# A decoder layer in fp32 on one core: order of the operands and the squares in the first projection, a second head in free PSUM banks, and page loads ahead of the V loads

## The chip, the core and the metric

The kernel runs on one core of a Trainium2 chip. Its engines are TensorE (PE, with its weight loads shown as PEld), VectorE (DVE), ScalarE (ACT), GpSimd (POOL) and SyncE (SP), which here only issues transfers. The metric is device time in microseconds (us) for one launch. Lower is better.

## The reference, cut to what matters

One inference step of one hybrid layer, for 512 prompt rows and 64 sample rows (8 sequences of 8), 576 columns in all in the kernel's layout:

```
z = rmsnorm(x, g_pre_mix) @ w_in                 # 2048 -> 5120: u, va, q, k, vb
u, va, q, k, vb = split(z)
a_out = gelu(u) * (w_s @ rmsnorm(gelu(va)) + b_s)
lam   = exp(sum(lq1*lk1)) - exp(sum(lq2*lk2)) + lam_init
o     = (softmax(q1 k1) - lam * softmax(q2 k2)) @ v      # prompt; samples read 16 cache pages each
mix   = concat(a_out, rmsnorm(o)) @ w_out
h     = x + rmsnorm(mix)
y     = h + rmsnorm((gelu(gate) * val) @ w_down)         # gate, val: conv of rmsnorm(h) @ w_up
```

rmsnorm needs the sum of squares of each column of x. The kernel multiplies the weights with the unscaled x (times the gain) and divides the product by the root R afterwards, so the squares are needed only when the first product leaves PSUM.

## The kernel before

Each fp32 operand is split into a high part (ACT, a copy to fp32r) and a low part (the rest). A product is three matmuls: high by high, low by high, high by low. For the input x there are 16 tiles of 128 rows, `xraw` -> `xh` (ACT, L767) and `xl` (DVE, L1285). A weight unit holds 8 tiles of 128 by 128. It is loaded into one of two `wraw` slots, its high part `wh` is written by ACT (L754 for the first four units, `w_split_hi` L392 later) and its low part `wl` by POOL (L1181 to L1186, `w_split_lo` L397). `unit_mm` (L412 to L414) is one unit: 8 tiles, two column halves, three matmuls, 48 in all. A head's q takes two units (0 and 1 for head 0), its k takes the next two (2 and 3), head 1 takes units 4 to 7, and so on for 8 heads; then come the V units, then eight batches.

The first stage. SP issues unit 0, then x in five parts (`X_PARTS`: 2, 2, 4, 4 and 4 tiles), with the constants `cs` and the lambda rows `lamin` after the first part and units 1 and 2 after the second and fourth. `cs` and `lamin` raise one semaphore, `c_landed`, and ACT and DVE wait for both. ACT makes the high parts of part q, then the squares of part q-1 (L761), then the high part of a unit. DVE makes the low parts of part q, then adds the squares of part q-1 (L1279). There are two buffers for squares, so ACT's square k waits for DVE's add k-2. The sum goes through TensorE (`sum_squares`, L1872) between units 2 and 3, ACT takes the root (L787), DVE the reciprocal (L1298). DVE then evacuates q (L1306) and k (L1309) of head 0 from banks 0 to 3, and TensorE begins head 1 in those same banks. ACT's order in `qk_act` is fixed: after q's evacuation it copies the sample columns (L794), and only then splits units 6 and 7. SP stores q after the evacuation and only then issues the load of unit 7.

The pages. `pg` has 8 slots. Page n of a batch waits until TensorE has used the page 8 places before it. In batch 0 TensorE runs `k_pages(0)`, a half unit, `k_pages(1)`, a half unit, then `k_pages(2)` (L1917), which needs pages 8 to 11; each `k_pages` is followed by the scores of the prompt (L1940). SP's order around that point:

```
v_loads(3, first_page=4)
sp.wait_ge(v_stored[0], 16 * H)
sp.wait_ge(v_stored[1], 16 * H)
token_loads(sp, sy, 0)      # ws, wb, V, vnew
bias_load(sp, sy, 0)        # bsb
batch_loads(0)              # pages 8 to 31, then 0 to 7 of the next batch
```

Of the kernel before, what the change touches and what calls it, by code (L numbers as in the profile page):

```python
# [37 lines left out]
P = 128  # L38
# [122 lines left out]
def build(nc, xT, wstream, kpages, vpages, state, ptab, consts, lams, wsT, wblk, bs,  # L161
# [56 lines left out]
    kT = sb("kT", [P, SEQ], at=c)  # L218
    qb = sb("qb", [P, H, 32], at=c)
    knew = sb("knew", [P, H, DT], at=c)  # L220
    loaded_early = c[0]
    V = sb("V", [P, 4, P], at=c)
    vnew = sb("vnew", [DT, H * P], at=c)
    ws = sb("ws", [P, P], at=c)
    wb = sb("wb", [NS, NS], at=c)
    bsb = sb("bsb", [P, P], at=c)
    S = sb("S", [P, PAGES * P + DT], at=c)
    En = sb("En", [DT, P], at=c)
    W = sb("W", [P, 1280], at=c)
# [92 lines left out]
    w_landed = [sem(f"w_landed{i}") for i in range(RAW + 2)]  # L322
    w_hi, w_lo, w_used = sem("w_hi"), sem("w_lo"), sem("w_used")

    c_landed, p_landed, ready = sem("c_landed"), sem("p_landed"), sem("consts_ready")
    x_landed = [sem(f"rows_landed{i}") for i in range(len(X_PARTS))]
    r_landed = x_landed[:4]
# [164 lines left out]
        q.dma_start(knew[:].rearrange("p h n -> p (h n)"),  # L492
                    ks_d[:, bass.ds(j, 1), :].rearrange("p a n -> p (a n)")).then_inc(sq_landed, 16)

    def token_loads(eng, q, j):

        wait_past(eng, s["gm_ready"], j)
        q.dma_start(ws[:], wsT[bass.ds(j, 1)].rearrange("a p n -> (a p) n")).then_inc(g_landed, 16)
        q.dma_start(wb[:], wblk[bass.ds(j, 1)].rearrange("a p n -> (a p) n")).then_inc(g_landed, 16)
        wait_past(eng, s["pv_ready"], j)  # L500
        q.dma_start(V[:], v_out[bass.ds(j, 1)].rearrange("a b p n -> p (a b) n")).then_inc(hv_landed, 16)
        wait_past(eng, s["spv_ready"], j)
        q.dma_start(vnew[:], vs_out[bass.ds(DT * j, DT)].rearrange("t h n -> t (h n)")).then_inc(sv_landed, 16)
# [10 lines left out]
    def _(sp):  # L514
# [7 lines left out]
        for q, (k0, k1) in enumerate(X_PARTS):  # L522
            sp.dma_start(xraw[:, k0:k1, :], xT[:, k0:k1, :]).then_inc(x_landed[q], 16)
            if q == 0:
                sp.dma_start(cs[:], consts).then_inc(c_landed, 16)
                sp.dma_start(lamin[:], lams.to_broadcast([P, 4, DH])).then_inc(c_landed, 16)
            if q in FIRST_UNITS:
                first_load(FIRST_UNITS[q])
        for u in (3, 4):
            first_load(u)  # L530

# [40 lines left out]
        sp.wait_ge(p_landed, 16)  # L572
        v_loads(2, first_page=0)
        head_loads(sp, sy, 0)
        v_loads(3, first_page=4)

        sp.wait_ge(v_stored[0], 16 * H)
        sp.wait_ge(v_stored[1], 16 * H)
        token_loads(sp, sy, 0)
        bias_load(sp, sy, 0)  # L580

        def batch_loads(j, last=False):
            for n in range(8, 12):
                page(n, j)
            for n in range(12, 24):
                page(n, j)
            for c in range(1, 3):
                for n in range(20 + 4 * c, 24 + 4 * c):
                    page(n, j)
            if not last:  # L590
                for n in range(8):
                    page(n, j + 1)
# [158 lines left out]
    def _(act):  # L751
# [2 lines left out]
            sc.activation(wh[:, u, :], wraw[:, u % RAW, :], ACT.Copy).then_inc(w_hi, 1)  # L754

        first_split_hi(0)
        act.wait_ge(c_landed, 32)
        def x_squares(k0, k1):
            for k in range(k0, k1):
                wait_past(act, x_acc, k - 1)  # L760
# [2 lines left out]
        for q, (k0, k1) in enumerate(X_PARTS):  # L763
            act.wait_ge(x_landed[q], 16)
            for k in range(k0, k1):

                sc.activation(xh[:, k, :], xraw[:, k, :], ACT.Copy, scale=cs[:, C_PRE + k:C_PRE + k + 1]  # L767
                              ).then_inc(x_hi, 1)
            if q:
                x_squares(*X_PARTS[q - 1])  # L770
            if q in FIRST_UNITS:
                first_split_hi(FIRST_UNITS[q])
            if q == 4:

                act.wait_ge(lam_sum, 2)
                sc.activation(lt[:, 2:4], lt[:, 0:2], ACT.Exp).then_inc(lam_exp, 1)
        first_split_hi(3)
        x_squares(*X_PARTS[-1])

        def qk_act(j):  # L780

            for t in range(2):
                w_split_hi(U_QK, 4 * t, 8, j)
                w_split_hi(U_QK, 4 * t + 1, 8, j)
                if type(j) is int and t == 0:
                    act.wait_ge(ssq_mm, 1)
                    sc.activation(halves(R[:]), tile_out(6), ACT.Sqrt, scale=1.0 / D, bias=EPS  # L787
                                  ).then_inc(sq_root, 1)
                act.wait_ge(q_evac, 2 * j + t + 1)
                act.wait_ge(pool_c, 2)  # L790
                for z in range(2):

                    o = 2 * DT * t + DT * z
                    sc.activation(  # L794
                        qbd[DH * z:DH * z + DH, :, bass.ds(2 * j + t, 1), o:o + DT].rearrange("p b a n -> p b (a n)"),
                        zt[0][DH * z:DH * z + DH, SEQ:T].rearrange("p (b n) -> p b n", b=DB),
                        ACT.Copy).then_inc(smp, 1)
                w_split_hi(U_QK, 4 * t + 2, 8, j)
# [13 lines left out]
        def batch(j, first=False, last=False):  # L812
# [46 lines left out]
            sc.activation(vq[:], vg[:], ACT.Square).then_inc(s["vsq_ready"], 1)  # L859

            wait_past(act, s["vaT_ready"], j)
            act.wait_ge(c_landed, 32)
            sc.activation(vaT[:], vg[:], ACT.Copy, scale=cs[:, bass.ds(C_VA + j, 1)]).then_inc(s["va_gained"], 1)
            act.wait_ge(s["vssq_ready"], j + 1)
            sc.activation(vr[:, 0:4], pb[:, 3, SSQ_COL:SSQ_COL + 4], ACT.Sqrt, scale=1.0 / HD, bias=EPS
# [15 lines left out]
            act.wait_ge(s["sss_ready"], j + 1)  # L881
            sc.activation(osq[:], pb[:, 4, 0:NS], ACT.Sqrt, scale=1.0 / HD, bias=EPS).then_inc(s["ssd_done"], 1)
            if not last:
                token_loads(act, sc, j + 1)
            act.wait_ge(s["u_evac"], j + 1)
            sc.activation(ug[:], ug[:], ACT.Gelu_apprx_tanh).then_inc(s["ugelu"], 1)
# [49 lines left out]

        def out_copy(t, m):

            act.wait_ge(c_landed, 32)
            sc.activation(mix_half(t, m), out_bank(t, m), ACT.Copy, scale=cs[:, C_POST + m:C_POST + m + 1]  # L940
                          ).then_inc(m_copied, 1)

# [107 lines left out]
        def conv_tap2(n, t):  # L1050
# [7 lines left out]
            act.wait_ge(ub_zero, 4)  # L1058
            act.wait_ge(st_in, 2 * n + 2 - t)
            wait_past(act, gv_done, n)  # L1060
            act.wait_ge(c_landed, 32)
            f_ = n + KF * t
            sc.activation(cv[t][:, 0:NC_], ubs[n % 2][t][:, 2:UB], ACT.Identity,
                          scale=cs[:, C_W + 4 * KF + f_:C_W + 4 * KF + f_ + 1],
# [196 lines left out]

    @block.vector
    def _(dve):
        dve.wait_ge(c_landed, 32)

        for z in range(2):
            v.tensor_tensor_reduce(out=lamin[:, 2 * z, :], in0=lamin[:, 2 * z, :], in1=lamin[:, 2 * z + 1, :],
                                   scale=1.0, scalar=0.0, op0=ALU.mult, op1=ALU.add,
                                   accum_out=lt[:, z:z + 1]).then_inc(lam_sum, 1)
        ch = Chain(dve, dve_c, 0)  # L1270
        ch.link(v.tensor_scalar(gsub[:], cs[:, C_SUB:C_SUB + 1], 1.0 - LAM_INIT, None, ALU.mult))
        def add_x_squares(k0, k1):
# [8 lines left out]
        for q, (k0, k1) in enumerate(X_PARTS):  # L1281
            dve.wait_ge(x_landed[q], 16)
            for k in range(k0, k1):
                dve.wait_ge(x_hi, k + 1)
                v.scalar_tensor_tensor(out=xl[:, k, :], in0=xraw[:, k, :], scalar=cs[:, C_PRE + k:C_PRE + k + 1],  # L1285
                                       in1=xh[:, k, :].bitcast(F32), op0=ALU.mult, op1=ALU.subtract
                                       ).then_inc(x_lo, 1)
            if q:
                add_x_squares(*X_PARTS[q - 1])
        add_x_squares(*X_PARTS[-1])  # L1290
        dve.wait_ge(lam_exp, 1)

        ch.link(v.tensor_tensor(lt[:, 0:1], lt[:, 3:4], lt[:, 2:3], ALU.subtract))
        ch.link(v.tensor_scalar(neglam[:], lt[:, 0:1], -LAM_INIT, None, ALU.add))
        ch.link(v.tensor_scalar(sgn[:], cs[:, C_SEL + 1:C_SEL + 2], neglam[:, 0:1], None, ALU.mult))
        ch.link(v.tensor_tensor(sgn[:], sgn[:], cs[:, C_SEL:C_SEL + 1], ALU.add))
        dve.wait_ge(sq_root, 1)
        v.reciprocal(R[:], R[:]).then_inc(R_ready, 1)  # L1298
        dve.wait_ge(R_ready, 1)
        Rh = halves(R[:])  # L1300

        def qk_evac(j):
            tile_done(dve, U_QK, 0, 4, j)
            wait_past(dve, q_stored, 16 * j)
            wait_past(dve, smp, 3 * j)
            v.tensor_tensor(halves(zt[0][:]), tile_out(0), Rh, ALU.mult).then_inc(q_evac, 1)  # L1306
            tile_done(dve, U_QK, 2, 4, j)
            wait_past(dve, k_stored, 16 * j)
            v.tensor_tensor(halves(zt[1][:]), tile_out(2), Rh, ALU.mult).then_inc(k_evac, 1)  # L1309

        qk_evac(0)
        with dve.Fori(1, H) as j:
            qk_evac(j)
        dve.wait_ge(q_stored, 16 * H)
        dve.wait_ge(k_stored, 16 * H)
# [548 lines left out]
    def _(pe):  # L1864
# [9 lines left out]
            m.then_inc(ssq_mm, 1)  # L1874

        tile_mm(0, U_QK, 0, k_sem=x_lo)
        unit_mm(2, U_QK, 2, xh, xl, 0, 8, True, False).then_inc(w_used, 1)
        sum_squares(6, (x_acc, KD, acc0))
        unit_mm(2, U_QK, 3, xh, xl, 8, 8, False, True).then_inc(w_used, 1)
        with pe.Fori(1, H) as j:  # L1880
            wait_past(pe, q_evac, j)
            tile_mm(0, U_QK, 0, 4, j)
            wait_past(pe, k_evac, j)
            tile_mm(2, U_QK, 2, 4, j)
# [440 lines left out]
```

## Time and profile before

| | us |
|---|---|
| median of three runs | 2623.59 (2622.09 to 2625.20) |
| the profiled execution, its own time | 2626.07 |
| its span, first to last instruction | 2624.3 |
| PE busy | 2536.9 (97% of the span) |
| DVE busy | 1463.3 (56%) |
| ACT busy | 1014.6 (39%) |
| POOL busy | 731.2 (28%) |
| load of one weight unit, issue to landing | 3.7 |

The mean granted TensorE clock is 0.990 of full speed. Positions below are us from the start of the span. A matmul of 288 columns starts 0.13 us after the one before it at the full clock of 2.4 GHz and 0.24 us after it at 1.2 GHz. In a timeline the bracket behind a row gives the idle time of the engine ahead of it and what ended it.

### The profile page before, as it was taken

The numbers are of one execution on the slowest core, as the hardware profiler recorded it, in microseconds if no ns is written. First come the engines' busy times: TensorE is split into PE (matmuls) and PEld (weight loads), VectorE is DVE, ScalarE is ACT, GpSimd is POOL, SyncE is SP. The second block draws the span as 40 slices with busy tenths as digits, with TensorE's granted clock in tenths as the row PEclk, the third lists the DMA queues.
The fourth block names the chain that finished last, engine by engine and source line by source line (L and its number), as shares of the span: only waits on it lengthen the run. The fifth ranks groups of instructions, "written<-read, shape, count | busy, mean of one in ns | idle before, by whom it ended". The sixth has DMA issues, their size and how long they took to land.

```text
span 2624.3 us, 49612 instructions
## 1 busy us (share of the span) xinstructions
PE 2536.9 (97%) x19608; PEld 2419.4 (92%) x19608; DVE 1463.3 (56%) x2100; ACT 1014.6 (39%) x1478; POOL 731.2 (28%) x547
## 2 busy tenths in 40 slices
PE   7999989999999999899999999999999999999997
PEld 6999967777778998899999999999999999999997
DVE  5000134445545378988888888888888302131347
ACT  5111133444444454444444444444444222222342
POOL 3333321212215500111111111111111433335774
PEclk9999999999999999999999999999999999999998
DMA  5333579999996663233333333333333442424654
GB/s 177 105 105 120 157 291 347 354 366 367 365 362 242 202 198 117 95 110 107 105 105 108 111 106 111 111 111 111 104 110 136 151 135 81 155 87 128 222 157 153
DMA packets 147367, 445.02 MB, mean 170 GB/s; under 512 B 17216, under 2 KB 39232, under 8 KB 145536
## 3 DMA queue, kind: packets, MB, share of 16 engines
q1 hardware_dynamic: 130608, 413.26, 46.7%
q10 hardware_dynamic: 15024, 24.70, 2.6%
q0 software_dynamic: 1568, 4.72, 0.4%
q8 instruction: 119, 1.95, 0.3%
q14 instruction: 48, 0.39, 0.0%
HBM read 406.05 MB, written 36.33 MB: 169 GB/s over the span
## 4 chain that ended last, share of the span: by engine, by line
PE 88%; DVE 5%; DMA 3%; issue 2%; SPq 1%; ACT 1%; ACTq 0%; POOL 0%; DVEq 0%; POOLq 0%
PE pb L2187 12%; PE pb L2189 12%; PE pb L2188 12%; PE pb L2213 7%; PE pb L2216 7%; PE pb L2215 7%; PE pb L412 6%; PE pb L414 5%; PE pb L413 5%; PE pb L2101 3%; PE pb L2103 3%; PE pb L2102 3%; PE pb L1981 2%; PE pb L1917 2%; DMA pg<-in_kpages 1%
## 5 line engine op out<-in xcount | busy, mean ns | idle before, releaser
L2187 PE MATMUL pb<-reg,uh 128*128 128x288 f32 x2408 | 713.2, 296 | 12.7 <-DVE reg L1576 5.4
L2189 PE MATMUL pb<-reg,ul 128*128 128x288 f32 x2408 | 711.9, 296 | 0.0
L2188 PE MATMUL pb<-reg,uh 128*128 128x288 f32 x2408 | 708.3, 294 | 0.0
L1035 ACT ACTIVATE uh<-ua 128x1024 fp32r<-128x1024 f32 x301 | 318.0, 1057 | 436.2 <-PE pb L2189 206.3
L2187 PEld LDWEIGHTS pb<-reg,uh 128*128 128x128 f32 x2408 | 452.8, 188 | 14.2 <-issue 10.8
L2188 PEld LDWEIGHTS pb<-reg,uh 128*128 128x128 f32 x2408 | 455.6, 189 | 0.0
L2189 PEld LDWEIGHTS pb<-reg,ul 128*128 128x128 f32 x2408 | 453.9, 188 | 0.0
L1637 DVE TENSOR_TENSOR ul<-ua,uh 128x1024 fp32r<-128x1024 f32 x301 | 367.4, 1221 | 103.6 <-ACT uh L1035 103.5
L412 PE MATMUL pb<-xh,wh 128*128 128x288 f32 x1280 | 387.1, 302 | 19.7 <-DVE xl L1285 18.5
L413 PE MATMUL pb<-xl,wh 128*128 128x288 f32 x1280 | 379.1, 296 | 0.0
L414 PE MATMUL pb<-xh,wl 128*128 128x288 f32 x1280 | 378.2, 295 | 0.0
L1259 POOL TENSOR_TENSOR ul<-ua,uh 128x1024 fp32r<-128x1024 f32 x120 | 291.8, 2440 | 288.9 <-ACT uh L1119 288.1
L397 POOL TENSOR_TENSOR wl<-wraw,wh 128x1024 fp32r<-128x1024 f32 x80 | 191.4, 2394 | 488.2 <-ACT wh L392 488.2
L2213 PE MATMUL pb<-xl,uh 128*128 128x288 f32 x1024 | 303.5, 296 | 4.1 <-POOL ul L1259 4.1
L2215 PE MATMUL pb<-xh,uh 128*128 128x288 f32 x1024 | 302.5, 295 | 0.0
L2216 PE MATMUL pb<-xl,ul 128*128 128x288 f32 x1024 | 302.0, 295 | 0.0
L1240 POOL COPY hs<-ub 128x2 f32<-128x2 f32 x88 | 52.9, 601 | 791.0 <-DVE ub L1698 631.6
L412 PEld LDWEIGHTS pb<-xh,wh 128*128 128x128 f32 x1280 | 242.1, 189 | 31.2 <-issue 23.4
L1119 ACT ACTIVATE uh<-ua 128x1024 fp32r<-128x1024 f32 x120 | 127.0, 1059 | 354.0 <-PE pb L2216 333.3
L414 PEld LDWEIGHTS pb<-xh,wl 128*128 128x128 f32 x1280 | 242.4, 189 | 0.0
L413 PEld LDWEIGHTS pb<-xl,wh 128*128 128x128 f32 x1280 | 242.2, 189 | 0.1
L392 ACT ACTIVATE wh<-wraw 128x1024 fp32r<-128x1024 f32 x80 | 84.8, 1059 | 320.4 <-PE pb L414 307.6
(254 smaller groups left out, 4368.9 us busy)
## 6 DMA issues: line engine op xcount, KB each, us to landing
ua<-in_wstream SPq DMA_DIRECT2D x292, 512.0 KB, 3.8
pg<-in_kpages SPq DMA_DIRECT2D x128, 512.0 KB, 5.7
pg<-in_vpages SPq DMA_DIRECT2D x128, 512.0 KB, 5.9
wraw<-in_wstream SPq DMA_DIRECT2D x82, 512.0 KB, 3.7
wraw<-in_wstream ACTq DMA_DIRECT2D x32, 512.0 KB, 6.3
wmore<-in_wstream SPq DMA_DIRECT2D x30, 512.0 KB, 3.9
g_d<-gv SPq DMA_DIRECT2D x44, 288.0 KB, 2.1
xh<-g_d SPq DMA_DIRECT2D x8, 1152.0 KB, 9.9
```

The costliest lines, as they stand in the source:

```text
L412: te.matmul(pb[:, bank + n, 0:TH], whk, hn, start=a0, stop=False)
L413: te.matmul(pb[:, bank + n, 0:TH], whk, ln, start=False, stop=False)
L414: m = te.matmul(pb[:, bank + n, 0:TH], wlk, hn, start=False, stop=z0)
L1035: sc.activation(uh[q % SLOTS][:], ua[src][:], ACT.Copy).then_inc(u_hi, 1)
L1259: pl.tensor_tensor(ul[dn_slot(q)][:], ua[DN_RAW[q % 4]][:], uh[dn_slot(q)][:].bitcast(F32), ALU.subtract).then_inc(u_lo, 1)
L1637: v.tensor_tensor(ul[q % SLOTS][:], ua[src][:], uh[q % SLOTS][:].bitcast(F32), ALU.subtract).then_inc(u_lo, 1)
L2187: te.matmul(out, whk, xhk, start=opens and k == 0, stop=False, skip_group_check=again)
L2188: te.matmul(out, whk, xlk, start=False, stop=False, skip_group_check=again)
L2189: m = te.matmul(out, wlk, xhk, start=False, stop=k == HK - 1, skip_group_check=again)
L2213: te.matmul(pb[:, b_ + n, 0:TH], whk, gh_[:, k, n * TH:(n + 1) * TH], start=r == r0 and kk == 0, stop=False)
L2215: te.matmul(pb[:, b_ + n, 0:TH], whk, gl_[:, k, n * TH:(n + 1) * TH], start=False, stop=False)
L2216: m = te.matmul(pb[:, b_ + n, 0:TH], wlk, gh_[:, k, n * TH:(n + 1) * TH], start=False, stop=r == r1 - 1 and kk == GRP - 1)
```

## The change

1. `lamin` gets a semaphore of its own, `lam_landed`, and its load is issued behind all of x. `c_landed` now stands for `cs` alone.
2. ACT makes the high parts of all 16 tiles of x (with units 1 and 2 between them), then squares 0 and 1, unit 3, squares 2 to 11, unit 4, squares 12 to 15, then the exponentials of lambda. DVE makes all low parts, then adds all squares, then does the lambda sums (L1267), the reciprocal of R, and the four small lambda operations (L1293 to L1296).
3. TensorE puts head 1 into banks 4 to 7. Its order is units 0 to 4, the sum of the squares (through banks 6 and 7), unit 5, a wait for the root, units 6 and 7; only head 2 returns to bank 0. `qk_evac` gets the bank as a parameter.
4. `ws`, `wb` and `bsb` move to the part of SBUF that is free early. `gate_loads` (ws, wb) and `bias_load` of batch 0 are issued ahead of `v_loads(3)`. Pages 8 to 11 are issued ahead of the wait for the V stores and the loads of `V` and `vnew`.

```diff
             sp.dma_start(xraw[:, k0:k1, :], xT[:, k0:k1, :]).then_inc(x_landed[q], 16)
             if q == 0:
                 sp.dma_start(cs[:], consts).then_inc(c_landed, 16)
-                sp.dma_start(lamin[:], lams.to_broadcast([P, 4, DH])).then_inc(c_landed, 16)
             if q in FIRST_UNITS:
                 first_load(FIRST_UNITS[q])
+        sp.dma_start(lamin[:], lams.to_broadcast([P, 4, DH])).then_inc(lam_landed, 16)
...
         v_loads(2, first_page=0)
         head_loads(sp, sy, 0)
+        gate_loads(sp, sy, 0)
+        bias_load(sp, sy, 0)
         v_loads(3, first_page=4)
-        sp.wait_ge(v_stored[0], 16 * H)
-        sp.wait_ge(v_stored[1], 16 * H)
-        token_loads(sp, sy, 0)
-        bias_load(sp, sy, 0)
         def batch_loads(j, last=False):
             for n in range(8, 12):
                 page(n, j)
+            if type(j) is int and j == 0:
+                sp.wait_ge(v_stored[0], 16 * H)
+                sp.wait_ge(v_stored[1], 16 * H)
+                token_loads(sp, sy, 0)
             for n in range(12, 24):
                 page(n, j)
...
-            if q:
-                x_squares(*X_PARTS[q - 1])
             if q in FIRST_UNITS:
                 first_split_hi(FIRST_UNITS[q])
-            if q == 4:
-                act.wait_ge(lam_sum, 2)
-                sc.activation(lt[:, 2:4], lt[:, 0:2], ACT.Exp).then_inc(lam_exp, 1)
+        x_squares(0, 2)
         first_split_hi(3)
-        x_squares(*X_PARTS[-1])
+        x_squares(2, 12)
+        w_split_hi(U_QK, 0)
+        x_squares(12, KD)
+        act.wait_ge(lam_sum, 2)
+        sc.activation(lt[:, 2:4], lt[:, 0:2], ACT.Exp).then_inc(lam_exp, 1)
...
-            if q:
-                add_x_squares(*X_PARTS[q - 1])
-        add_x_squares(*X_PARTS[-1])
+        add_x_squares(0, KD)
+        dve.wait_ge(lam_landed, 16)
+        for z in range(2):
+            v.tensor_tensor_reduce(...).then_inc(lam_sum, 1)
+        dve.wait_ge(sq_root, 1)
+        v.reciprocal(R[:], R[:]).then_inc(R_ready, 1)
         dve.wait_ge(lam_exp, 1)
...
         qk_evac(0)
-        with dve.Fori(1, H) as j:
+        qk_evac(1, 4)
+        with dve.Fori(2, H) as j:
             qk_evac(j)
...
         tile_mm(0, U_QK, 0, k_sem=x_lo)
-        unit_mm(2, U_QK, 2, xh, xl, 0, 8, True, False).then_inc(w_used, 1)
+        tile_mm(2, U_QK, 2)
+        unit_mm(4, U_QK, 4, xh, xl, 0, 8, True, False).then_inc(w_used, 1)
         sum_squares(6, (x_acc, KD, acc0))
-        unit_mm(2, U_QK, 3, xh, xl, 8, 8, False, True).then_inc(w_used, 1)
-        with pe.Fori(1, H) as j:
+        unit_mm(4, U_QK, 5, xh, xl, 8, 8, False, True).then_inc(w_used, 1)
+        pe.wait_ge(sq_root, 1)
+        tile_mm(6, U_QK, 6)
+        with pe.Fori(2, H) as j:
```

## Rows read from the trace of the kernel before

**Rows 1.** Timeline of PE, first stage: start, duration, line, [idle before <- releaser].

```profile
11.28 0.58 PE L412 MATMUL pb<-xh,wh 128*128 128x288 f32 x1 [11.28 <-DVE xl L1285]
...
30.37 0.61 PE L412 MATMUL pb<-xh,wh 128*128 128x288 f32 x1 [4.91 <-DVE xl L1285]
...
42.20 1.13 PE L1872 MATMUL pb<-acc,ones 128*128 128x288 f32 x4
...
49.95 0.40 PE L412 MATMUL pb<-xh,wh 128*128 128x288 f32 x1 [0.25 <-DVE zt L1306]
...
62.71 0.29 PE L414 MATMUL pb<-xh,wl 128*128 128x288 f32 x1
```

**Rows 2.** Busy time of each engine by stretch, two stretches with the granted clock.

```profile
28.35:35.18 6.83, 4.81 (x20) 4.81 (x21) 6.52 (x8) 4.53 (x9) 1.36 (x1) 0.50 0.29 79
...
357.20:362.90 5.70, 5.68 (x23) 1.70 (x24) 0.41 (x1) 0.60 (x1) 0.00 (x0) 0.50 0.76 297
```

**Rows 3.** Timeline of PE around batch 0's page waits and batch 1's.

```profile
342.41 0.37 PE L1940 MATMUL pb<-kT,qT 64*128 64x128 f32 x1
...
357.21 3.64 PE L1917 MATMUL pb<-pg,qb 128*32 128x512 f32 x16 [5.05 <-DMA pg<-in_kpages]
...
418.15 1.92 PE L1917 MATMUL pb<-pg,qb 128*32 128x512 f32 x16 [2.19 <-DMA pg<-in_kpages]
```

**Rows 4.** DMA from 0 to 60 us: GB/s in 1.5 us slices, issues with time to landing.

```profile
GB/s 0 128 356 381 101 287 441 432 430 430 405 436 425 383 145 0 0 0 0 0 85 265 11 0 0 0 115 235 5 0 259 90 0 32 231 270 56 194 316 3
...
cs<-in_consts SPq DMA_DIRECT2D x1, 217.5 KB, 4.9
lamin<-in_lams SPq DMA_DIRECT2D x1, 128.0 KB, 7.0
```

**Rows 5.** The last part of x, line L523: its issue, and its time to landing.

```profile
L523 SPq DMA_DIRECT2D xraw<-in_xT x1: 442/442/442, 8.6 to 8.6; - x1
...
DMA to landing us min/median/max: 13.1/13.1/13.1
```

**Rows 6.** Timeline of ACT, first stage.

```profile
9.39 2.88 ACT L767 ACTIVATE xh<-xraw,cs 128x576 fp32r<-128x576 f32 x4 [3.56 <-DMA lamin<-in_lams]
...
26.24 1.04 ACT L754 ACTIVATE wh<-wraw 128x1024 fp32r<-128x1024 f32 x1
...
44.52 0.65 ACT L787 ACTIVATE R<-pb 128x576 f32<-128x576 f32 x1
49.85 0.53 ACT L794 ACTIVATE qbd<-zt 64x64 f32<-64x64 f32 x2 [4.68 <-DVE zt L1306]
```

**Rows 7.** Timeline of DVE, first stage.

```profile
24.00 3.34 DVE L1279 TENSOR_TENSOR acc<-acc,sq 128x576 f32<-128x576 f32 x4
28.04 4.46 DVE L1285 SCALAR_TENSOR_TENSOR xl<-xraw,cs,xh 128x576 fp32r<-128x576 f32 x4 [0.71 <-ACT xh L767]
...
45.27 3.75 DVE L1298 RECIPROCAL R<-R 128x576 f32<-128x576 f32 x1 [1.36 <-ACT R L787]
```

**Rows 8.** Timeline of POOL, first stage.

```profile
27.35 2.35 POOL L1186 TENSOR_TENSOR wl<-wraw,wh 128x1024 fp32r<-128x1024 f32 x1 [10.53 <-ACT wh L754]
...
51.54 2.40 POOL L397 TENSOR_TENSOR wl<-wraw,wh 128x1024 fp32r<-128x1024 f32 x1 [5.29 <-ACT wh L392]
```

**Rows 9.** Timeline of PE: two idle gaps in the feed-forward stage and the matmuls behind them.

```profile
1077.28 0.37 PE L2187 MATMUL pb<-reg,uh 128*128 128x288 f32 x1 [2.78 <-DVE reg L1576]
...
1084.17 0.58 PE L2187 MATMUL pb<-reg,uh 128*128 128x288 f32 x1 [3.47 <-DVE u L1687]
```

**Rows 10.** Timeline of SP's queue at the start of batch 0.

```profile
345.51 1.53 SPq L508 DMA_DIRECT2D bsb<-in_bs  x1
348.00 8.08 SPq L563 DMA_DIRECT2D pg<-in_kpages  x8
```

**Rows 11.** Busy time by stretch, batches 1 and 2: PE, PEld, DVE, ACT, POOL, clock, DMA share, GB/s.

```profile
392.80:451.30 58.50, 54.95 (x507) 41.75 (x506) 27.35 (x66) 23.97 (x54) 11.62 (x9) 1.00 0.95 353
451.30:507.90 56.60, 54.96 (x507) 41.76 (x506) 27.46 (x66) 23.98 (x54) 11.58 (x9) 1.00 0.96 366
```

More of the change, by code:

```diff
@@ L220, in build @@
     knew = sb("knew", [P, H, DT], at=c)
+    ws = sb("ws", [P, P], at=c)
+    wb = sb("wb", [NS, NS], at=c)
+    bsb = sb("bsb", [P, P], at=c)
     loaded_early = c[0]
@@ L223, in build @@
     vnew = sb("vnew", [DT, H * P], at=c)
-    ws = sb("ws", [P, P], at=c)
-    wb = sb("wb", [NS, NS], at=c)
-    bsb = sb("bsb", [P, P], at=c)
     S = sb("S", [P, PAGES * P + DT], at=c)
@@ L323, in build @@
     w_hi, w_lo, w_used = sem("w_hi"), sem("w_lo"), sem("w_used")
+    lam_landed = sem("lam_landed")
     c_landed, p_landed, ready = sem("c_landed"), sem("p_landed"), sem("consts_ready")
@@ L493, in head_loads, with gate_loads @@
                     ks_d[:, bass.ds(j, 1), :].rearrange("p a n -> p (a n)")).then_inc(sq_landed, 16)
-    def token_loads(eng, q, j):
+    def gate_loads(eng, q, j):
         wait_past(eng, s["gm_ready"], j)
@@ L499, in token_loads @@
         q.dma_start(wb[:], wblk[bass.ds(j, 1)].rearrange("a p n -> (a p) n")).then_inc(g_landed, 16)
+    def token_loads(eng, q, j):
         wait_past(eng, s["pv_ready"], j)
@@ L756, in _ @@
         first_split_hi(0)
-        act.wait_ge(c_landed, 32)
+        act.wait_ge(c_landed, 16)
         def x_squares(k0, k1):
@@ L768, in _ @@
                               ).then_inc(x_hi, 1)
-            if q:
-                x_squares(*X_PARTS[q - 1])
             if q in FIRST_UNITS:
                 first_split_hi(FIRST_UNITS[q])
-            if q == 4:
-                act.wait_ge(lam_sum, 2)
-                sc.activation(lt[:, 2:4], lt[:, 0:2], ACT.Exp).then_inc(lam_exp, 1)
+        x_squares(0, 2)
         first_split_hi(3)
-        x_squares(*X_PARTS[-1])
+        x_squares(2, 12)
[3 more added lines that the diff above has]
+        sc.activation(lt[:, 2:4], lt[:, 0:2], ACT.Exp).then_inc(lam_exp, 1)
         def qk_act(j):
             for t in range(2):
-                w_split_hi(U_QK, 4 * t, 8, j)
+                if type(j) is not int or t:
+                    w_split_hi(U_QK, 4 * t, 8, j)
                 w_split_hi(U_QK, 4 * t + 1, 8, j)
@@ L861, in batch @@
             wait_past(act, s["vaT_ready"], j)
-            act.wait_ge(c_landed, 32)
+            act.wait_ge(c_landed, 16)
             sc.activation(vaT[:], vg[:], ACT.Copy, scale=cs[:, bass.ds(C_VA + j, 1)]).then_inc(s["va_gained"], 1)
@@ L883, in batch @@
             if not last:
+                gate_loads(act, sc, j + 1)
                 token_loads(act, sc, j + 1)
@@ L937, in out_copy @@
         def out_copy(t, m):
-            act.wait_ge(c_landed, 32)
+            act.wait_ge(c_landed, 16)
             sc.activation(mix_half(t, m), out_bank(t, m), ACT.Copy, scale=cs[:, C_POST + m:C_POST + m + 1]
@@ L1060, in conv_tap2 @@
             wait_past(act, gv_done, n)
-            act.wait_ge(c_landed, 32)
+            act.wait_ge(c_landed, 16)
             f_ = n + KF * t
@@ L1263, in _ @@
     def _(dve):
[L1264 to L1269, printed above, removed]
+        dve.wait_ge(c_landed, 16)
         ch = Chain(dve, dve_c, 0)
@@ L1287, in _ @@
                                        ).then_inc(x_lo, 1)
-            if q:
-                add_x_squares(*X_PARTS[q - 1])
-        add_x_squares(*X_PARTS[-1])
+        add_x_squares(0, KD)
+        dve.wait_ge(lam_landed, 16)
+        for z in range(2):
+            v.tensor_tensor_reduce(out=lamin[:, 2 * z, :], in0=lamin[:, 2 * z, :], in1=lamin[:, 2 * z + 1, :],
+                                   scale=1.0, scalar=0.0, op0=ALU.mult, op1=ALU.add,
+                                   accum_out=lt[:, z:z + 1]).then_inc(lam_sum, 1)
+        dve.wait_ge(sq_root, 1)
+        v.reciprocal(R[:], R[:]).then_inc(R_ready, 1)
         dve.wait_ge(lam_exp, 1)
@@ L1296, in _, with qk_evac @@
         ch.link(v.tensor_tensor(sgn[:], sgn[:], cs[:, C_SEL:C_SEL + 1], ALU.add))
-        dve.wait_ge(sq_root, 1)
-        v.reciprocal(R[:], R[:]).then_inc(R_ready, 1)
         dve.wait_ge(R_ready, 1)
         Rh = halves(R[:])
-        def qk_evac(j):
+        def qk_evac(j, bank_=0):
             tile_done(dve, U_QK, 0, 4, j)
@@ L1305, in qk_evac @@
             wait_past(dve, smp, 3 * j)
-            v.tensor_tensor(halves(zt[0][:]), tile_out(0), Rh, ALU.mult).then_inc(q_evac, 1)
+            v.tensor_tensor(halves(zt[0][:]), tile_out(bank_), Rh, ALU.mult).then_inc(q_evac, 1)
             tile_done(dve, U_QK, 2, 4, j)
             wait_past(dve, k_stored, 16 * j)
-            v.tensor_tensor(halves(zt[1][:]), tile_out(2), Rh, ALU.mult).then_inc(k_evac, 1)
+            v.tensor_tensor(halves(zt[1][:]), tile_out(bank_ + 2), Rh, ALU.mult).then_inc(k_evac, 1)
         qk_evac(0)
-        with dve.Fori(1, H) as j:
+        qk_evac(1, 4)
+        with dve.Fori(2, H) as j:
             qk_evac(j)
```

## The prediction, made before the changed kernel ran

> **What bounds the kernel now.** I read the page first: TensorE is busy 97% of the span, so only time in which it idles or runs at the lower clock can be won. Then I asked for TensorE's waits up to 90 us and around the start of the batches, and read each gap in the timelines. In the first stage TensorE starts at 11.28, stands still 4.91 us before 30.37 for the last part of x's low halves, and is then fed without a gap over 0.3 us: the two units of head 1 run from 49.95 to 62.71 [rows 1]. That is 96 matmuls, 0.134 us apart, so one unit is 6.4 us and unit 6 starts at 62.85. After the gap the clock is at the lower of its two levels, 1.2 of 2.4 GHz, until 35.18 [rows 2]. The second place is batch 0: `k_pages(2)` waits 5.05 us for page 11 and then takes 3.64 us instead of 1.92 [rows 3], with the clock at the lower level until 362.9 [rows 2]. These two places are what the change touches.
>
> **Parts 1 and 2, the first stage.** Each time is from the span's start.
>
> *Loads.* The first high part waited for `lamin` from 5.83 to 9.39 [rows 6]; `cs`, issued 0.47 us before it, lands 2.1 us sooner relative to its own issue, so at about 6.75 [rows 4]. The first high part therefore moves to about 6.8: 2.6 us. For the later parts of x, what `lamin` holds up in the queue is between 0.3 us (its 128 KB at 430 GB/s) and 2.6 us (9.32 less 6.75, if nothing else landed meanwhile). The rate falls to 101 and 287 GB/s in the slices from 6 to 9 us [rows 4], which is 1.7 us lost plus the bytes: I take 2.0. The last part of x, issued at 8.65 and landed 13.1 us later [rows 5], comes at 19.7 instead of 21.75.
>
> *Operands.* ACT makes a tile's high part in 0.69 us and four in 2.8 [rows 6], so tiles 12 to 15 get theirs from 19.7 to 22.5, where before the first began at 27.18, behind squares and a unit split. Unit 2's split stands just before them, at 18.4, and POOL, which takes 2.35 for a low part [rows 8], runs it from 19.5 to 21.85. DVE collides with that: the four low parts that began at 28.04 ended 2.8 us after POOL's operation did [rows 7, 8], the first held until POOL was through. So DVE's last low part ends at 21.85 + 2.8 = 24.65, and TensorE's products with it at 25.5. The same point was at about 35.8 before (30.37 plus four tiles of 1.44 us at the lower clock, the last at the full one): 10.3 us sooner. Units 2 and 3 follow to 38.3.
>
> *Squares.* They are now behind all of that: the adds begin at 24.6. POOL's low part of unit 3 runs 24.65 to 27.0, and add 1 is held to 27.6. From there ACT and DVE alternate at 0.86 us (four adds in 3.34 [rows 7]); square 11, and behind it on ACT the split of unit 4, comes at 35.1, its low part is ready at 38.65. TensorE waits 0.3 us, nothing more. Unit 4 lasts to 45.05. The adds end at 41.7, hidden by it with 3.3 us to spare; the lambda sums and the exponential follow, and unit 5 is split by 45.85, just at its turn. With this cover gone (squares over 3.3 us later) every further us is a us of TensorE.
>
> *The root, and what is late next.* Before, the sum's matmuls started at 42.20 and unit 4 began 7.75 us later, of which unit 3 covered nearly all [rows 1]. Now: sum 45.05 to 46.2, root 0.65, reciprocal 3.75 [rows 6, 7], four small lambda operations about 0.8 that are now behind it, evacuation 0.76, ending at 52.4. But ACT waits for this evacuation before it copies sample columns (0.53, [rows 6]) and splits unit 6 (1.04), and POOL needs 2.40 after it [rows 8]: unit 6 can start at 56.5. TensorE has done unit 5 by 52.2. It waits about 3.8 us. Unit 7's load, behind the same evacuation on SP, lands 3.7 us after it and is split before unit 6 is through, so it costs nothing. Unit 6 moves from 62.85 to 56.5: 6.3 us.
>
> *The clock in that gap.* A gap of 3.47 us left the clock low (first matmul 0.58), one of 2.78 did not (0.37) [rows 9]; 3.8 is on the side of the first, as are 4.91 and 5.05. From 30.37 the lower level lasted to 35.18 and from 357.21 to 362.9, of which half is lost: 2.4 to 2.8 us. I take 2.6. The Trainium skill ("TensorE: Matmul & The Clock Gate", Part 1) says that the point at which the clock changes differs from run to run of one kernel; by that page the gap could also pass at the full clock, which is a rival below. Net for the first stage: 6.3 - 2.6 = 3.7 us.
>
> The collision of DVE and POOL has a page as well: the Trainium skill ("SBUF — State Buffer", SBUF: two separate sides) makes it an exclusive lock that goes to whoever started first, so that POOL would also wait for a DVE add with two inputs. The rows show only DVE waiting. By the page the low parts of units 3 and 4 could each start up to 0.76 us late, and the sum below would be 10.1 instead of 10.9.
>
> **Part 3.** Without the other banks unit 4 could not start before the evacuation; its cost is nil, since the matmuls are the same. Its gain is in the times above.
>
> **Part 4, batch 0.** SP issued the token and bias loads until 347.0 and pages 8 to 11 only from 348.00 [rows 10], though TensorE had used pages 0 to 3 at 342.4, where the scores behind them begin [rows 3]. Page 11 landed just before 357.2, 9.1 us after the first issue. Now the first goes out at 342.5, page 11 lands at about 351.6, and `k_pages(2)` is due at 352.1. The wait of 5.05 goes, and with it the lower clock: 1.7 us in `k_pages(2)` [rows 3] and about 0.8 in what follows it; half of the stretch of 5.70 at the lower clock [rows 2] would be 2.85, and I count 2.5. What moves: `V` and `vnew` are now behind four page issues and a wait for TensorE, 2 us later, and are needed only some 45 us on, at the start of the first stretch of [rows 11]; ws, wb and bsb add 2.4 us of SP time ahead of a V unit's load of 3.7, and TensorE takes 6.4 for a unit and has another in hand. Pages 12 to 15 are issued from 348.2, behind `V`, land by 357.5 and are due at 358.5. Lower bound 5.05 (clock stays low anyway), upper 7.55. I take 7.2, near the upper end, as the clock falls only with a gap.
>
> **Sum.** 3.7 + 7.2 = 10.9 us. The profiled execution took 2626.07, 1.8 over its span of 2624.3, and would take 2615.2; the median of the runs is 2623.6, so 2612.7. Everything behind the two places is fed by TensorE's own progress and shifts with it.
>
> **Rivals.**
>
> *The clock holds in the new gap* (20%): 6.3 + 7.2 = 13.5, time 2610.1. For it: 3.8 is close to 3.47. Against: none of the gaps from 3.47 up that I read left it high.
>
> *The batches give part of it back* (15%). DMA is busy 95% and moves 353 GB/s in batch 1 and 366 in batch 2, and batch 1 has a page wait of 2.19 [rows 3, 11]. If the pages cannot follow 7 us sooner, this wait grows to about 6 with a lower clock behind it: total gain 5 to 6, time 2618. For it: batch 1 is 1.9 us longer than batch 2. Against: batch 2 moves 366 GB/s where batch 1 moves 353, so the queue has room there.
>
> *The first stage gains nothing* (8%). Squares come over 3.3 us late, and unit 4 and the root with them; with 4 us of that, only part 4 is left: 2616.4.
>
> *Slower* (4%). The pages now run just behind their slots in every batch, and the wait before `k_pages(2)`, 2.19 in batch 1, passes the 3.5 us at which the clock falls. Each such batch costs about 3.5 more of waiting and 2.6 of clock, 6 in all. Two cancel the gain, three make it slower: 2631 with four. For it: DMA at 95%. Against: batch 2 shows what a batch settles to, 56.60 for 54.96 of work.
>
> The forecast itself has 50%, with 2611 to 2615 as its own range; 3% is for the rest.
>
> **How the numbers follow.** A measurement of this kernel can tell about 0.2%, 5.2 us, from no change. Faster than 2618.4: the forecast, the first and third case, most of the second: 0.87. Same: the rest of the second and a small gain: 0.08. Slower: 0.05. The range reaches below to the clock case less 1.6 us for the runs' own spread, 2608.5, and above past the second and third case, 2618.5.
>
> **What would show it.** TensorE starts near 8.9; its products with the last tile end at 25 to 26; it waits 3 to 5 us ahead of unit 6 for POOL's low part, starting that unit near 56.5, at the lower clock; no page wait at batch 0, whose third page group takes 1.92; batch 1's page wait at 1 to 3 us. The prediction is wrong if ACT's squares with POOL's locks run slower than 0.86 each, so that unit 4 waits by us, if the page waits grow, or if the gap ahead of unit 6 is much longer.

## The result, and the profile after

| | before | after |
|---|---|---|
| median of the runs, us | 2624.86 (6 runs, 2622.09 to 2626.18) | 2614.62 (6 runs, 2612.61 to 2616.43) |
| profiled execution, own time | 2626.07 | 2614.37 |
| its span | 2624.3 | 2612.4 |

By its median the changed kernel is 10.2 us faster. The ratio that was worked out from the runs is 0.9966, 95% interval 0.9956 to 0.9976, which is 8.9 us (6.3 to 11.5). The prediction was 2612.7, with 2608.5 to 2618.5 as its range, and faster. The kernel before was timed again beside the changed one, so its median here is 1.3 us above the one that the prediction started from. A later measurement (the last experiment) gave 0.9972, 0.9960 to 0.9983.

The timeline of TensorE in the first stage, changed kernel; the columns are those of [rows 1]:

```profile
8.80 0.58 PE L413 MATMUL pb<-xh,wh 128*128 128x288 f32 x1 [8.80 <-DVE xl L1286]
...
22.06 0.40 PE L413 MATMUL pb<-xh,wh 128*128 128x288 f32 x1 [1.32 <-DVE xl L1286]
...
38.56 0.40 PE L413 MATMUL pb<-xh,wh 128*128 128x288 f32 x1 [0.25 <-POOL wl L398]
...
45.06 1.13 PE L1877 MATMUL pb<-acc,ones 128*128 128x288 f32 x4
...
56.33 0.37 PE L413 MATMUL pb<-xh,wh 128*128 128x288 f32 x1 [3.76 <-POOL wl L398]
...
64.32 0.30 PE L413 MATMUL pb<-xh,wh 128*128 128x288 f32 x1
```

The 4.91 us ahead of the last part of x are 1.32. Units 0 to 4 are done where the sum of the squares starts, at 45.06; before, units 0 to 2 were done at 42.20. The new gap is where it was expected: 3.76 us ahead of unit 6, ended by POOL's low part. Unit 6 starts at 56.33 instead of 62.85, 6.5 us sooner; the last row is the start of unit 7.

The chain that ends in it, on ACT, DVE and POOL, from their timelines:

```profile
46.23 0.65 ACT L792 ACTIVATE R<-pb 128x576 f32<-128x576 f32 x1 [1.74 <-PE pb L1877]
52.16 0.53 ACT L799 ACTIVATE qbd<-zt 64x64 f32<-64x64 f32 x2 [5.27 <-DVE zt L1310]
52.71 1.06 ACT L393 ACTIVATE wh<-wraw 128x1024 fp32r<-128x1024 f32 x1
```

```profile
20.09 4.10 DVE L1286 SCALAR_TENSOR_TENSOR xl<-xraw,cs,xh 128x576 fp32r<-128x576 f32 x4 [0.95 <-ACT xh L772]
...
46.92 3.75 DVE L1296 RECIPROCAL R<-R 128x576 f32<-128x576 f32 x1 [4.91 <-ACT R L792]
```

```profile
18.95 2.44 POOL L1192 TENSOR_TENSOR wl<-wraw,wh 128x1024 fp32r<-128x1024 f32 x1 [5.85 <-ACT wh L759]
24.16 2.67 POOL L1192 TENSOR_TENSOR wl<-wraw,wh 128x1024 fp32r<-128x1024 f32 x1 [2.77 <-ACT wh L759]
...
53.84 2.34 POOL L398 TENSOR_TENSOR wl<-wraw,wh 128x1024 fp32r<-128x1024 f32 x1 [8.19 <-ACT wh L393]
```

The split of unit 6 (ACT, 52.71) stands behind the sample columns, which wait for the evacuation, and its low part ends at 56.2. ACT had been idle for 5.27 us before that.

The clock in and behind the gap (busy time by stretch, columns as in [rows 11]):

```profile
52.60:57.18 4.58, 0.85 (x6) 0.88 (x7) 0.18 (x1) 1.83 (x3) 2.34 (x1) 0.99 0.57 179
57.18:60.59 3.41, 3.41 (x17) 3.41 (x15) 0.76 (x1) 0.60 (x3) 2.37 (x1) 0.51 0.85 235
```

It fell, as forecast, but not within the gap: unit 6 runs at the upper level for its first 0.8 us and then at the lower one for 3.41 us, and not for 5. Unit 7 starts 7.99 us behind unit 6, where a unit takes 6.40 at the upper level: 1.6 us is lost. From there to the V units the changed kernel is 4.9 us ahead.

Batch 0, TensorE and then SP's queue (before: [rows 3, 10]):

```profile
347.50 1.92 PE L1925 MATMUL pb<-pg,qb 128*32 128x512 f32 x16 [0.28 <-DMA pg<-in_kpages]
...
354.47 1.92 PE L1925 MATMUL pb<-pg,qb 128*32 128x512 f32 x16 [0.76 <-DMA pg<-in_kpages]
```

```profile
336.24 0.55 SPq L558 DMA_DIRECT2D out_vs<-vt  x1
337.88 4.05 SPq L567 DMA_DIRECT2D pg<-in_kpages  x4
342.04 0.40 SPq L505 DMA_DIRECT2D V<-out_v  x1
342.48 0.51 SPq L507 DMA_DIRECT2D vnew<-out_vs  x1
343.98 3.69 SPq L567 DMA_DIRECT2D pg<-in_kpages  x4
```

The third page group waits 0.28 us instead of 5.05 and takes 1.92 instead of 3.64. It starts 9.7 us ahead of the kernel before, of which 4.9 came from the first stage; the fourth group starts 11.5 us ahead (354.47 instead of 366.02). By the start of the output projection the lead is 11.4 (table below).

### The profile page after: what moved, and what is told of

Its sections match the earlier page's. It is cut to its first block, busy times and chain, and to the rows that moved or that the text cites. A ratio compares the mean times of both kernels' runs of the same rounds, so it can differ in the third digit from the quotient of the medians.

```text
span 2612.4 us, 49600 instructions
## 1 busy us (share of the span) xinstructions
PE 2532.2 (97%) x19608; PEld 2417.1 (93%) x19608; DVE 1463.4 (56%) x2100; ACT 1015.6 (39%) x1478; POOL 731.4 (28%) x547
## 4 chain that ended last, share of the span: by engine, by line
PE 87%; DVE 4%; DMA 3%; issue 2%; SPq 1%; ACT 1%; POOL 1%; ACTq 0%; DVEq 0%; POOLq 0%
PE pb L2195 12%; PE pb L2197 12%; PE pb L2196 12%; PE pb L2221 7%; PE pb L2224 7%; PE pb L2223 7%; PE pb L413 5%; PE pb L415 5%; PE pb L414 5%; PE pb L2109 3%; PE pb L2111 3%; PE pb L2110 3%; PE pb L1989 2%; DMA pg<-in_kpages 2%; PE pb L1925 1%
```

## The experiments

Positions are from each run's own profile. "Lead" is by how much the first matmul of the output projection, the first work of TensorE behind the eight batches, comes sooner than in the kernel before. Each ratio is to the kernel before on the same chip. Its medians there were 2624.86 beside the changed kernel, 2623.65 beside the first four experiments, 2623.50 beside the next four and 2622.42 beside the last two. There is one profile of the kernel before, of an execution of 2626.07 us, which is 1.2 to 3.6 us above these medians; so leads come out larger than what the medians show.

| run | median | ratio, 95% interval | unit 6 starts | wait of page group 3 | lead |
|---|---|---|---|---|---|
| before | 2624.86 | | 62.85 | 5.05 | |
| after | 2614.62 | 0.9966 (0.9956 to 0.9976) | 56.33 | 0.28 | 11.4 |
| first stage alone | 2620.62 | 0.9988 (0.9979 to 0.9998) | 56.38 | 5.10 | 3.9 |
| batch 0 alone | 2617.52 | 0.9980 (0.9971 to 0.9989) | 62.60 | none | 8.9 |
| no gap | 2609.62 | 0.9945 (0.9932 to 0.9959) | 52.47 | 1.45 | 18.0 |
| one set of banks | 2620.98 | 0.9990 (0.9980 to 0.9999) | | none | 3.1 |
| banks alone, batch 0 changed | 2617.66 | 0.9978 (0.9968 to 0.9988) | 62.79 | 0.76 | 6.7 |
| lambda load back | 2616.33 | 0.9970 (0.9958 to 0.9982) | 58.82 | 0.21 | 10.0 |
| V ahead of the pages | 2618.48 | 0.9979 (0.9969 to 0.9988) | 56.67 | 4.04 | 9.2 |
| no gap, V later | 2607.50 | 0.9938 (0.9924 to 0.9952) | 52.81 | none | 15.8 |
| last part first | 2608.08 | 0.9946 (0.9933 to 0.9960) | 52.61 | 0.18 | 17.4 |
| after, once more | 2614.86 | 0.9972 (0.9960 to 0.9983) | 56.38 | 0.60 | 11.9 |

**First stage alone.** The changed kernel with the old order at batch 0.

```diff
         head_loads(sp, sy, 0)
-        gate_loads(sp, sy, 0)
-        bias_load(sp, sy, 0)
         v_loads(3, first_page=4)
+        sp.wait_ge(v_stored[0], 16 * H)
+        sp.wait_ge(v_stored[1], 16 * H)
+        gate_loads(sp, sy, 0)
+        token_loads(sp, sy, 0)
+        bias_load(sp, sy, 0)
...
-            if type(j) is int and j == 0:
-                sp.wait_ge(v_stored[0], 16 * H)
-                sp.wait_ge(v_stored[1], 16 * H)
-                token_loads(sp, sy, 0)
```

> The changed first stage with the order of loads of the kernel before at batch 0. Theory (the two parts add up, and each is worth what its place shows): TensorE as in the changed kernel up to the batches, 4.9 us ahead of the kernel before; batch 0's page wait back at about 5 us with the lower clock behind it, end 4.9 us before the kernel before's. Rival (the batches are bound by their transfers and swallow an earlier start of TensorE): the lead shrinks to under 2 us by the end of the batches.

The wait is back at 5.10 us, the clock falls behind it, and the lead of 4.9 survives that place. At the end of the batches it is 3.9: the theory holds with 1 us given back, which is more than nothing and far from the rival's "under 2". The runs' median is 3.0 us below the kernel before, with an interval from 0.5 to 5.5.

**Batch 0 alone.** The kernel before with only the page, gate and bias loads reordered.

> The first stage of the kernel before with the changed order of loads at batch 0. Theory: no lead until 340 us, then 6.5 us, 2 of it by the clock that no longer falls, and 6.5 at the end. Rival (most of the saved wait comes back later as a longer page wait in batch 1 or 2): a lead of 6.5 behind batch 0 and under 4 at the end of the batches.

Batch 0 is left with a lead of 8.0 and the output projection starts 8.9 sooner; the runs' median says 6.1 (forecast 6.5). The rival is out. The two parts together come to 9.2 us by the medians, the whole change to 10.2 and 7.6 in its two measurements: they add up, as far as this can tell.

**No gap.** ACT splits unit 6 and SP loads unit 7 ahead of their waits for q's evacuation.

```diff
                 w_split_hi(U_QK, 4 * t + 1, 8, j)
+                if first_head:
+                    w_split_hi(U_QK, 2, 8, j)
                 if type(j) is int and t == 0:
                     act.wait_ge(ssq_mm, 1)
...
+            if type(j) is int:
+                w_load(U_QK, 2, 4, j)
             sp.wait_ge(q_evac, j + 1)
```

> The changed kernel with ACT's split of unit 6 ahead of its wait for the evacuation of q of head 0, and SP's load of unit 7 ahead of the same wait. Theory (the 3.76 us ahead of unit 6 are the chain evacuation, sample columns, high part, low part, and the lower clock for 3.4 us behind it costs 1.7): both go, unit 6 starts at 52.2 and the kernel is 5.5 us faster than the changed one, 16 to 17 below the kernel before. Rival (the root comes late in any case and only moves the wait to unit 8, which needs head 0's evacuation): the gap moves behind unit 7, gain under 2 us.

ACT and POOL now do both units back to back while the sum of the squares goes on:

```profile
42.22 1.99 ACT L393 ACTIVATE wh<-wraw 128x1024 fp32r<-128x1024 f32 x2
```

```profile
43.34 4.75 POOL L398 TENSOR_TENSOR wl<-wraw,wh 128x1024 fp32r<-128x1024 f32 x2 [4.76 <-ACT wh L393]
```

Unit 6 starts at 52.47, straight behind unit 5; no gap comes behind unit 7 either, and the clock stays at the upper level to the end of the batches. Batch 0 starts 5.4 us ahead of the changed kernel, as forecast from 3.76 and 1.7 (the two are 3.86 and 1.6). The time is 14.0 us below the kernel before, against 10.2 and 7.6 for the changed one, and not 16 to 17. Part of that may be the third page group, which waits 1.45 us here: one issue of a V store takes SP 1.92 us instead of 0.6, and page 8 goes out 1.6 us after its slot is free. Why that issue took longer I have not found. The two moves, on ACT and on SP, were not tried apart.

**One set of banks.** The changed kernel with head 1 in banks 0 to 3 again.

```diff
         tile_mm(2, U_QK, 2)
-        unit_mm(4, U_QK, 4, xh, xl, 0, 8, True, False).then_inc(w_used, 1)
         sum_squares(6, (x_acc, KD, acc0))
-        unit_mm(4, U_QK, 5, xh, xl, 8, 8, False, True).then_inc(w_used, 1)
-        pe.wait_ge(sq_root, 1)
-        tile_mm(6, U_QK, 6)
-        with pe.Fori(2, H) as j:
+        with pe.Fori(1, H) as j:
...
         qk_evac(0)
-        qk_evac(1, 4)
-        with dve.Fori(2, H) as j:
+        with dve.Fori(1, H) as j:
```

> The changed kernel with head 1 back in banks 0 to 3: TensorE runs units 0 to 3, the sum of the squares, then unit 4 behind the evacuation. Theory (the second set of banks is what lets TensorE use its head start of 10 us): TensorE idles from 38 to about 42 for the adds and from 43 to 49.5 for the root, at the lower clock behind it, so unit 4 starts 0 to 1 us before where it did in the kernel before, and the first stage gains nothing; 6.5 us in all, from batch 0. Rival (the gain of the first stage is the earlier operands alone, the banks are incidental): 10 to 11 us as in the changed kernel.

```profile
41.92 2.29 PE L1876 MATMUL pb<-acc,ones 128*128 128x288 f32 x4 [3.45 <-DVE acc L1280]
50.68 0.60 PE L413 MATMUL pb<-xh,wh 128*128 128x288 f32 x1 [6.47 <-DVE zt L1310]
```

TensorE reaches the end of unit 3 some 11 us sooner than before and then has nothing to do: 3.45 us for the adds, 6.47 for the root. The rival is out. Unit 4 starts at 50.68, 0.7 us after its place in the kernel before, not 0 to 1 before it: I had not counted that the sum itself runs at the lower clock (2.29 us for 1.13). The lower clock lasts until 54.8, and unit 8 starts 2.6 us later than in the kernel before (78.22 for 75.65). The first stage has turned from a gain into a loss. Batch 0 gives 7.3 us, so that the lead is 4.8 behind its fourth page group, and 3.1 is left at the end of the batches. The runs' median is 2.7 us below the kernel before, and not 6.5.

**Banks alone.** The old order of loads, operands and squares, with head 1 in banks 4 to 7 and batch 0 as changed.

> The first stage of the kernel before in its order of loads, operands and squares, with only the second head in banks 4 to 7; batch 0's loads in the changed order. Theory (banks without the earlier operands save nothing but the 0.25 us ahead of unit 4, since TensorE reaches the end of unit 3 only when the root is nearly done): unit 6 starts 0 to 0.5 us ahead of the kernel before, the whole is as the run with batch 0's part alone, 6 us. Rival (the banks are the gain): 10 us.

Unit 6 starts at 62.79, as in the kernel before (62.85), and the median is 5.8 us lower, as with batch 0's part alone (6.1). The second set of banks by itself gives nothing, and the earlier operands without it less than nothing: the 6.5 us exist only together.

**Lambda load back.** The load of the lambda rows in its old place, with the new semaphore.

```diff
             if q == 0:
                 sp.dma_start(cs[:], consts).then_inc(c_landed, 16)
+                sp.dma_start(lamin[:], lams.to_broadcast([P, 4, DH])).then_inc(lam_landed, 16)
-        sp.dma_start(lamin[:], lams.to_broadcast([P, 4, DH])).then_inc(lam_landed, 16)
```

> The changed kernel with the lambda rows' load issued in its old place behind the constants, still with a semaphore of its own. Theory (the load holds the queue for 2.55 us): every part of x lands 2.5 us later than in the changed kernel, TensorE starts at most 1 us later but ends the products of the last tile and starts unit 6 2.5 us later, the kernel is 2.5 us slower than the changed one. Rival (only the common semaphore cost time): no difference.

Unit 6 starts at 58.82, 2.5 us later. The DMA rate in 1.5 us slices shows the hole, here and, below it, gone in the changed kernel:

```profile
GB/s 0 123 399 354 70 263 427 443 424 430 412 425 435 386 191 0 87 257 16 0 139 210 0 0 0 0 0 0 254 112 0 0 0 0 0 0 0 246 300 25
```

```profile
GB/s 0 142 355 410 407 443 442 406 436 390 445 430 193 272 19 268 82 0 38 292 19 0 0 0 0 0 87 273 5 0 0 0 0 0 0 202 257 87 147 290
```

From 6 to 9 us the rate is 70 and 263 GB/s with the load and 407 and 443 without it. A load of 128 KB, the same 1 KB row to 128 partitions, costs the queue 2.5 us, where its bytes at 430 GB/s would take 0.3. It is over a third of what unit 6 gained. The 2.5 us are read from the profile; the runs' medians, 7.2 us below the kernel before here and 10.2 and 7.6 for the changed kernel, cannot tell them.

**V ahead of the pages.** The wait for the V stores and the loads of V and vnew ahead of pages 8 to 11; the gate and bias loads stay early.

> The changed kernel with the wait for the V stores and the loads of V and vnew ahead of pages 8 to 11, as before; ws, wb and bsb stay early. Theory (each us by which page 8 is issued later is a us of TensorE at the third page group): page 8 goes out at 341 instead of 337.9, TensorE waits 3 to 3.5 us there, and if the clock falls 2.5 more; 3 to 6 us slower than the changed kernel. Rival (the early gate and bias loads were the gain): under 1 us slower.

The pages go out at 342.08 instead of 337.88, the third group waits 4.04 us and the clock falls. So the place of the pages is the gain, not the early gate loads. By the medians 5.0 us of the gain is left, where the changed kernel has 10.2 and 7.6: it costs some 3 to 5 us. The lead at the end of the batches is only 2.2 below the changed kernel's, since this profile has nearly no page waits in the later batches. TensorE's waits for pages from 365 to 800 us (us in total, times, longest), this kernel and then the changed one with the first stage alone:

```profile
PE pb L1925 <- DMA pg<-in_kpages: 0.5, 2, 0.3
```

```profile
PE pb L1925 <- DMA pg<-in_kpages: 4.7, 8, 1.4
```

**No gap, V later.** V and vnew behind page 15.

```diff
-            for n in range(12, 24):
+            for n in range(12, 16):
                 page(n, j)
+            if type(j) is int and j == 0:
+                sp.wait_ge(v_stored[0], 16 * H)
+                sp.wait_ge(v_stored[1], 16 * H)
+                token_loads(sp, sy, 0)
+            for n in range(16, 24):
+                page(n, j)
```

> The kernel without the gap ahead of unit 6, and in batch 0 V and vnew behind page 15. Theory (pages 12 to 15 come 1 us sooner, so the wait ahead of the fourth page group goes): that wait, 0.4 to 0.8, is zero; 0.5 us better than without the move, which the runs' times cannot tell but the profile can. Rival (the pages are bound by the transfer rate, V's 0.26 MB must come in any case): the wait stays or moves to the V pages.

The wait ahead of the fourth group stays, 0.59 us: the rival is right, the move does nothing that can be seen. (The third group does not wait here, since page 8 goes out 0.3 us after its slot is free.) The kernel is the fastest by its median, 16.0 us below the kernel before, and cannot be told from the one without the move.

**Last part first.** On top of that, other places for three unit splits on ACT.

```diff
-            if q in FIRST_UNITS:
-                first_split_hi(FIRST_UNITS[q])
+            if q == 1:
+                first_split_hi(1)
+        first_split_hi(2)
         x_squares(0, 2)
         first_split_hi(3)
-        x_squares(2, 12)
+        x_squares(2, 9)
         w_split_hi(U_QK, 0)
-        x_squares(12, KD)
+        x_squares(9, 13)
+        w_split_hi(U_QK, 1, 8, 0)
+        x_squares(13, KD)
...
-                w_split_hi(U_QK, 4 * t + 1, 8, j)
+                if not first_head:
+                    w_split_hi(U_QK, 4 * t + 1, 8, j)
```

> The kernel without the gap and with V behind page 15, and on ACT also: the split of unit 2 behind the high parts of the last tiles, unit 4 split after square 8, unit 5 after square 12. Theory (POOL's low part of unit 2 holds DVE's first low part of the last four tiles for 1.1 us, which is TensorE's 1.3 us gap before that tile; unit 4 then comes 0.24 us late): both gaps go, TensorE starts unit 6 1.5 us earlier, at about 51. Rival (the held time moves with POOL's operation: the adds or unit 5 come late instead): the gap reappears ahead of the sum of the squares or of unit 5, and unit 6 starts within 0.5 us of where it did.

DVE's four low parts take 3.00 us instead of 4.06 in the kernel that this one was made from, and TensorE's gap ahead of the last part of x is 0.21 instead of 1.31. But POOL's operation has moved onto the path: TensorE waits for it ahead of unit 2, and DVE's copy of the first square is held by it (one row each of TensorE, DVE and POOL):

```profile
25.52 0.40 PE L413 MATMUL pb<-xh,wh 128*128 128x288 f32 x1 [1.04 <-POOL wl L1209]
```

```profile
23.61 2.17 DVE L1294 COPY acc<-sq 128x576 f32<-128x576 f32 x1 [0.45 <-ACT sq L775]
```

```profile
23.08 4.96 POOL L1209 TENSOR_TENSOR wl<-wraw,wh 128x1024 fp32r<-128x1024 f32 x2 [9.89 <-ACT wh L768]
```

Unit 6 starts at 52.61 against 52.81. The rival is right in that the held time moves and nothing is won, though most of the gap comes back ahead of unit 2 (1.04 us) and only 0.17 ahead of the sum of the squares.

**After, once more.** The changed kernel, unedited.

> The changed kernel once more, unedited, beside the run above on one chip. Theory: 10 us below the kernel before, unit 6 at 56.3 behind a gap of 3.76. Rival for the clock (its fall in that gap is a matter of where the gap falls): the clock stays at the upper level or the lower stretch has another length than 3.4 us, and the run is up to 2 us better or 1 worse.

7.6 us below the kernel before, with an interval that overlaps the first one. The gap is 3.75 us at the same place. The clock has fallen before its end this time (unit 6's first matmul takes 0.58, against 0.37 above), and the lower level ends at 59.2, again some 3.4 us after it began. But part of that lies in the gap, where TensorE has nothing to lose: unit 7 starts 7.74 us behind unit 6, so 1.3 us is lost and not 1.6. The clock fell in all five profiles that have the gap. The rival, that it might hold, found nothing for it.

## Why the prediction was right, point by point

**Loads.** Mis-sized: I took 2.0 us for the lambda load in the queue, between 0.3 and 2.6. It was 2.5, near the upper bound. The low rate in the two slices was the right sign; I should have taken the landings (`cs` 6.75, `lamin` 9.32) at their word.

**Operands and squares.** Right in mechanism and nearly in size. The last tile's products end at 25.4 (25.5 forecast), the wait ahead of unit 4 is 0.25 (0.3), the sum starts at 45.06 (45.05). DVE's low part was held by POOL as forecast, and the eleven adds from 24.67 took 11.41 us, the first of them 2.78 instead of 0.76. Of the page in the Trainium skill ("SBUF — State Buffer", SBUF: two separate sides), which makes the hold mutual and takes in copies within SBUF: the last experiment but one shows a copy of 0.45 us held to 2.17, and in the changed kernel POOL's operation that starts at 24.16, 0.4 us before DVE's copy ends, takes 2.67 instead of 2.34 to 2.44. So the trace agrees, but by 0.3 us once, not by 0.76 twice.

**The root and the gap.** Right: 3.76 us forecast as 3.8, unit 6 at 56.33 for 56.5. The experiment without the gap shows that its cause is the order on ACT and SP and not the root; it moves both at once and does not say what each is worth.

**The clock.** Right that it falls, in this and in the four other profiles that have the gap; mis-sized in what it costs. I took 2.6 us from two stretches of 4.8 and 5.7 us behind gaps of 5 us; behind this shorter gap 1.6 was lost in the first profile and 1.3 in the last. Nor did unit 6 start at the lower clock in the first profile; in the last it did. So the first stage gave 4.9 us and not 3.7, by the profile.

The reason that I gave, 3.8 us on the far side of a limit between 2.78 and 3.47, does not hold. [rows 9] has two gaps of the feed-forward stage. In the profile of the changed kernel the second of them stands at 1072.70, and another one, 2.65 us at 1071.07 in the kernel before and passed at the upper level there, stands at 1059.61 (the second block has the columns of [rows 11]):

```profile
1059.61 0.37 PE L2195 MATMUL pb<-reg,uh 128*128 128x288 f32 x1 [2.84 <-DVE reg L1581]
...
1072.70 0.37 PE L2195 MATMUL pb<-reg,uh 128*128 128x288 f32 x1 [3.48 <-DVE u L1692]
```

```profile
1060.80:1064.00 3.20, 3.20 (x15) 3.20 (x15) 3.20 (x3) 1.86 (x2) 0.00 (x0) 0.50 0.00 0
1072.70:1078.00 5.30, 5.29 (x40) 5.30 (x41) 4.69 (x11) 3.25 (x5) 0.92 (x6) 1.00 0.87 297
```

Here the clock falls 1 us behind the gap of 2.84 and stays up behind the one of 3.48, while in the kernel before it stayed up behind 2.65 and 2.78 and fell in 3.47. In that range the length of a gap alone does not say whether the clock falls, and the 3.5 us in the case of a slower kernel is no limit either. That 3.8 us was enough in five profiles of five is what was measured; that I counted on it from two gaps was in part luck.

**Batch 0.** 7.2 forecast, 6.6 found behind the fourth page group (7.7 in the run with batch 0 alone, where neither group waits): the third group still waits 0.28 and the fourth 0.76, which I had at nothing. Pages 8 to 11 took 9.5 us from first issue to last landing and not 9.1, and went out 0.4 us after their slots were free, because SP had been at the V stores until 336.8 and then took 1.1 us for the first page.

**The sum.** 3.7 + 7.2 = 10.9 forecast, 4.9 + 6.6 = 11.5 by the profile up to batch 0, and 10.2 (8.9 by the ratio) and 7.6 by the runs. The first stage alone and batch 0 alone gave 3.0 and 6.1 by their medians. The forecast value leans on luck: the first stage was 1.2 us better than forecast and batch 0 was 0.6 worse, and half of the one cancelled against the other.

**The rivals.** The clock did not hold. The batches did not give back as much as the second case wants (5 us): from the fourth page group of batch 0 to the output projection the lead shrinks by 0.2 us in the changed kernel, by 1.2, 1.3 and 1.7 in three other profiles (first stage alone; no gap, V later; one set of banks), and grows or stays in the rest. The first stage did gain. The slower case did not occur: the longest page wait behind batch 0 in the changed kernel is 1.4 us, in batch 1, where 1 to 3 was the sign. Its sum was also wrong: at 6 us for each batch, 2631 goes with three such batches, and four give 2637.

## What to carry to other kernels

When work is moved ahead so that one engine gets further before a late result, look for what else stands in line behind that result on the other engines: here TensorE got two units further, and a split and a load that did not need the result waited for it on ACT and SP. Moving these two ahead of the wait was worth as much again as the first stage's gain, 5.4 us by the profiles and 4 to 6 by the medians. Two edits that each give nothing or lose (a second set of banks, operands ahead of squares) can be the whole gain together, so undo them one at a time before dropping either. A small broadcast load in front of large ones is to be priced by its landing, not by its bytes: here 2.5 us against 0.3.

## What the runs showed of the hardware that I had not expected

The total of TensorE's page waits behind batch 0 differs by several us between profiles of nearly the same program: 0.5 us in one, 4.7 in another, 3.3 in the kernel before (its longest is in [rows 3]). It gives or takes more than the edits at batch 0 are off by, and the lead at the end of the batches has to be read with it. I have not found what decides it.

The clock behind a gap of 2.8 to 3.5 us fell or stayed up in different places of two profiles whose order of work in that stage is the same (the point on the clock above). A profile of one execution is therefore good for reading a place, and less good for adding up a kernel to a microsecond.
